# Low parts of the w_mlp_out weights: a negative from ScalarE and an adding transfer inside the SBUF, in place of VectorE's subtraction

## What is computed

```python
def _mlp(h, w_in, w_out):
    a = jnp.square(jax.nn.relu(h @ w_in))     # w_in 1024 x 4096
    return a @ w_out                          # w_out 4096 x 1024
```

## Time and profile before

| | |
|---|---|
| median of 3 runs | 1048.42 us |
| lowest, highest | 1047.06, 1050.18 us |
| the profiled execution | 1049.96 us |
| its span in the trace | 1048.0 us, 12487 instructions |
| mean granted TensorE clock | 0.977 |

### The profile page before, as it was taken

How to read it: one execution, slowest core, us unless ns; L and a number is a source line. 1 busy time by engine, 2 the same in 40 slices (tenths; PEclk the granted TensorE clock), 3 DMA queues, 4 the chain that set the end, 5 groups by cost and what they waited for, 6 DMA issues and landing times.

```text
span 1048.0 us, 12487 instructions
## 1 busy us (share of the span) xinstructions
PE 999.5 (95%) x4663; PEld 834.3 (80%) x4663; DVE 516.0 (49%) x815; ACT 407.4 (39%) x586; POOL 56.8 (5%) x40
## 2 busy tenths in 40 slices
PE   8916999999999999899999998999999999999998
PEld 7805888888888888688888887888888888888887
DVE  4804442313444151878888888574441314444221
ACT  7503432112334131656666666444441213433110
POOL 1100000000000000212222222000000000000000
PEclk9967999999999999999999999999999999999999
DMA  6652423232232323122222222142323233232231
GB/s 223 97 61 73 121 80 121 81 121 80 81 120 80 121 81 84 47 71 72 70 70 70 70 90 80 43 119 81 120 81 121 81 107 94 80 119 82 81 121 40
DMA packets 82667, 95.13 MB, mean 91 GB/s; under 512 B 3065, under 2 KB 61482, under 8 KB 82634
## 3 DMA queue, kind: packets, MB, share of 16 engines
q1 hardware_dynamic: 80954, 89.95, 27.4%
q0 software_dynamic: 1680, 4.72, 3.1%
HBM read 89.94 MB, written 4.72 MB: 90 GB/s over the span
## 4 chain that ended last, share of the span: by engine, by line
PE 89%; DVE 5%; another core or an unknown queue 3%; ACT 1%; issue 1%; DMA 1%; SPq 0%; DVEq 0%
PE bank L1081 28%; PE bank L1083 28%; PE bank L1082 28%; PE bank L1255 2%; PE bank L1285 1%; DVE w_low L717 1%; DMA work<-in_x_dram 1%; DVE h_low_buf L726 1%; DVE a_low_buf L726 1%; DVE work L738 1%; ACT w_high L457 1%; DVE work L908 0%; DVE neg_max L944 0%; DVE work L854 0%
## 5 line engine op out<-in xcount | busy, mean ns | idle before, releaser
L717 DVE TENSOR_TENSOR w_low<-raw,w_high 128x2048 fp32r<-128x2048 f32 (+1 forms) x75 | 163.3, 2177 | 268.0 <-ACT w_high L457 267.9
L1081 PE MATMUL bank<-h_high_buf,w_high 128*128 128x512 f32 x640 | 252.7, 395 | 0.0
L457 ACT ACTIVATE w_high<-raw 128x2048 fp32r<-128x2048 f32 (+1 forms) x77 | 140.1, 1819 | 288.8 <-PE bank L1083 254.7
L1083 PE MATMUL bank<-h_high_buf,w_low 128*128 128x512 f32 x640 | 250.5, 391 | 0.0
L1082 PE MATMUL bank<-h_low_buf,w_high 128*128 128x512 f32 x640 | 250.5, 391 | 0.0
L1081 PE MATMUL bank<-a_high_buf,w_high 128*128 128x512 f32 x528 | 207.6, 393 | 3.8 <-DVE a_low_buf L726 3.7
L1083 PE MATMUL bank<-a_high_buf,w_low 128*128 128x512 f32 x528 | 206.5, 391 | 0.0
L1082 PE MATMUL bank<-a_low_buf,w_high 128*128 128x512 f32 x528 | 206.3, 391 | 0.0
L1083 PEld LDWEIGHTS bank<-h_high_buf,w_low 128*128 128x128 f32 x640 | 120.8, 189 | 25.5
L1081 PEld LDWEIGHTS bank<-h_high_buf,w_high 128*128 128x128 f32 x640 | 121.1, 189 | 25.0 <-DVE h_low_buf L726 0.4
L1082 PEld LDWEIGHTS bank<-h_low_buf,w_high 128*128 128x128 f32 x640 | 121.1, 189 | 24.5
(11 more groups left out here) (130 smaller groups left out, 872.4 us busy)
## 6 DMA issues: line engine op xcount, KB each, us to landing
raw<-in_w_mlp_in_dram SPq DMA_DIRECT2D x32, 1024.0 KB, 5.5
raw<-in_w_mlp_out_dram SPq DMA_DIRECT2D x32, 1024.0 KB, 5.0
raw<-in_w_kv_dram SPq DMA_DIRECT2D x16, 512.0 KB, 4.0
raw<-in_w_q_dram SPq DMA_DIRECT2D x8, 512.0 KB, 5.3
raw<-in_w_o_dram SPq DMA_DIRECT2D x3, 1024.0 KB, 4.9
bias_by_distance<-work POOLq DMA_DIRECT2D x1, 2560.0 KB, 54.1
work<-in_x_dram SPq DMA_DIRECT2D x4, 512.0 KB, 5.3
work<-bias_by_distance POOLq DMA_DIRECT2D x8, 256.0 KB, 2.9
```

Source lines behind the costliest of these rows:

```text
L457: act.activation(w_high_buf[s][:, 0:cols], raw[s][:, 0:cols], ACT.Copy).then_inc(w_high, 1)
L717: dve.tensor_tensor(w_low_buf[s][:, 0:cols], raw[s][:, 0:cols], f32(w_high_buf[s][:, 0:cols]), ALU.subtract)\
L1081: pe.matmul(acc, w_hi, m_hi, start=start, stop=False)
L1083: return pe.matmul(acc, w_lo, m_hi, start=False, stop=stop)
```

## The change

For the 32 units of w_mlp_out (places 8 to 15 in each half), VectorE no longer subtracts. ScalarE, right behind its copy of the high part, writes the negative of the high part into the low buffer; it is the same copy with scale -1. GpSimd waits for that and issues one transfer inside the SBUF which adds the whole raw unit onto the low buffer: -high + raw. VectorE waits for the transfer and then writes one number into `low_cell`, only to count `w_low` in the old order. Two semaphores take turns, by the parity of the unit's index among the 32. The loops over these units are written out, since the index must be a number. GpSimd issues the 16 transfers of layer 0 after the bias rows' write and before its work for the heads, those of layer 1 at the end of its program.

```diff
+        low_cell = sb("low_cell", [1, 32])
...
+        neg_high = sem("neg_high")
+        low_added = [sem(f"low_added{i}") for i in range(2)]
...
+        def out_index(u):
+
+            for l in range(2):
+                d = u - U_MLP[l]
+                if 0 <= d < 32 and d % 16 >= 8:
+                    return 16 * l + 8 * (d // 16) + d % 16 - 8
+            return None
...
+            def add_lows(l):
+                for half in range(2):
+                    for q in range(8):
+                        u = U_MLP[l] + 16 * half + 8 + q
+                        n = out_index(u)
+                        pool.wait_ge(neg_high, n + 1)
+                        pool.dma_start(w_low_buf[u % 2][:, :], raw[u % 2][:, :], accum_op=ALU.add).then_inc(low_added[n % 2], 16)
+
+            add_lows(0)
             pool.wait_ge(w_used, U_HEAD)
...
             split_low(POOL_UNITS[1 + H])
+            add_lows(1)
...
+            def split_unit(u):
+
+                split_high(u, u % 2, landed(u))
+                if out_index(u) is not None:
+                    act.activation(w_low_buf[u % 2][:, :], raw[u % 2][:, :], ACT.Copy, scale=-1.0).then_inc(neg_high, 1)
...
-                    with act.Fori(first, 4) as i:
+                    with act.Fori(first, 3) as i:
                         for j in range(2):
                             split_high(u0 + 1 + j + 2 * i, (u0 + 1 + j) % 2, landed(u0 + 1 + j, i))
                             hidden(c0 + 2 * j + 4 * i, 2 * j + 4 * i)
+                    for j in range(2):
+                        split_unit(u0 + 7 + j)
+                        hidden(c0 + 2 * j + 12, 2 * j + 12)
...
+            def low_unit(u):
+
+                n = out_index(u)
+                if n is None:
+                    split_low(u, u % 2)
+                else:
+                    dve.wait_ge(low_added[n % 2], 16 * (n // 2 + 1))
+                    dve.memset(low_cell[:, n:n + 1], 0.0).then_inc(w_low, 1)
...
-                            with dve.Fori(0, 2) as r:
-                                for j in range(2):
-                                    u = u0 + 8 + 4 * f + 1 + j
-                                    split_low(u + 2 * r, u % 2)
+                            for q in range(4):
+                                low_unit(u0 + 9 + 4 * f + q)
```

More of the change, by code:

```diff
@@ L521, in mlp @@
                             for q in range(4):
-                                split_high(u + q, (u + q) % 2, landed(u + q))
+                                split_unit(u + q)
                                 if q in (1, 2):
@@ L534, in mlp @@
                         else:
-                            with act.Fori(0, 2) as r:
-                                for j in range(2):
-                                    split_high(u + j + 2 * r, (u + j) % 2, landed(u + j, r))
+                            for q in range(4):
+                                split_unit(u + q)
             act.wait_ge(consts_ready, 1)
@@ L784, in mlp @@
                         first = 1
-                    with dve.Fori(first, 4) as i:
+                    with dve.Fori(first, 3) as i:
                         for j in range(2):
@@ L788, in mlp @@
                             hidden(u0 + j + 2 * i, n0 + j + 2 * i, c0 + 2 * j + 4 * i, 2 * j + 4 * i, j)
+                    for j in range(2):
+                        low_unit(u0 + 7 + j)
+                        hidden(u0 + j + 6, n0 + j + 6, c0 + 2 * j + 12, 2 * j + 12, j)
                     for f in range(NF):
@@ L792, in mlp @@
                             for q in range(3):
-                                split_low(u0 + 13 + q, (u0 + 13 + q) % 2)
+                                low_unit(u0 + 13 + q)
                         elif l == 1 and half == 1:
                             for q in range(4):
-                                split_low(u0 + 9 + q, (u0 + 9 + q) % 2)
+                                low_unit(u0 + 9 + q)
                                 if q in (1, 2):
```

## The result

The changed kernel takes 1099.22 us (median of 4 runs, 1096.71 to 1100.43) against 1048.05 (4 runs): **1.048 times as long, interval 1.046 to 1.051**, some 51 us. The forecast was 1135 in a range of 1063 to 1205. The span grew from 1048.0 to 1098.6 us, by 50.6.

The account below looks back on a forecast made before the run. TensorE's own rate, 10.88 us a unit, was taken as the bound, with a new chain of 12.7 us exceeding it. Stalls 68.6, clock 8 and overlap 10 gave 87 us on 1048.4: 1135 us, range 1063 to 1205.

Parts of the forecast that it names:

- The bound and the slack: w_mlp_out stages: only TensorE's rate decides, 10.88 us a unit; VectorE's 73 us of subtractions lie in 6.6 us idle slack.
- T: Issue to landing of one 1 MB adding transfer in SBUF, taken as 8.7 us; the new chain decides from 6.8.
- The chain: From TensorE's release to the next unit's start: copy, negative, transfer, memset, 4.1 + T, 12.7 us in all against 10.88.
- Units 8 and 9: First two w_mlp_out units of each half: stalls of 3.9 and 6.8 us, the latter from hidden chunks queued behind VectorE's wait.
- Steady units: Units 11 to 15 of each half: stalls of 1.8, 0.7, 1.1, 0.7 and 1.1 us; unit 10 none.
- The second half of layer 0: Squares and norm sums between units 13 and 14 make unit 14 about 6 us late; this half loses 20.3 us, others 16.1.
- The clock: TensorE at 1.2 GHz after five longer stalls (four before units 9, one before unit 14): 1.6 us each, 8 us.
- Overlap: Transfers beside the load of unit u+2, by up to 2.9 us: 10 us taken, between 0 and 30.
- The sum: Whole kernel: stalls 68.6, clock 8 and overlap 10 make 87 us on the 1048.4 median, 1135 us.
- The third rival: Transfers hidden altogether, T at or below 4: 1048 us, only 2 us left at units 9; chance 0.03.
- The fourth rival: Faster: third rival plus a gain at the 34.71 us start-up load wait at 48.83; below 1045, at best 1019; chance 0.02.

Follow-up runs that it names:

- The copying transfers: The changed kernel with the addition (accum_op=ALU.add) left out, so the transfers copy raw over the low buffer: 1054.64 us, ratio 1.0055.
- the best of the changed kernels: The changed kernel with VectorE's subtraction kept for units 8 and 9 and the other 24 transfers cut in two column halves: 1057.03 us, ratio 1.0081.

## Why the prediction was right, and where it was off

- **The bound and the slack**: right. The removed 73 us of VectorE gave nothing back, ScalarE's pass costs nothing by itself, and the change is decided by one chain against 10.88 us.
- **T**: the mis-sized term. I took 2.1 + 2 x 3.3 = 8.7; the median is 6.9. The factor of two was right (5.2 against 2.7 us of the engines), but a pass inside the SBUF takes 2.7 us and not the 3.3 of a load, and the part that doesn't grow with size is 1.5 (4.2 - 2.7) and not 2.1: 1.5 and twice 2.7 are 6.9. Of the 32 transfers 7 took 8.4 to 10.4.
- **The chain** 4.1 + T: the parts are 0.05, then 1.83 for the copy and 1.90 for the negative (I had 1.92 for each), 0.29 for GpSimd to get going (I had 0.05), and 0.11 from the landing to TensorE's first product (0.15): 4.2. With 6.9 it is 11.1. The form was right, and the small errors nearly cancelled.
- **Units 8 and 9**: the places, their cause and their order were right. TensorE stood for 2.5 us before unit 8 (3.9 forecast, 2.2 by the formula at 6.9) and 2.8 before unit 9 (6.8; unit 9 started 15.6 behind unit 8 where the formula at 6.9 has 15.95, but 1.9 of that time went into unit 8 itself at its lower clock). Moving the wait shows the queue's part, 16.7 us.
- **Steady units**: forecast 1.8, 0.7, 1.1, 0.7 and 1.1, 5.4 a half; measured 2.0 in the first half. That is T again.
- **The second half of layer 0**: 4.2 us above an ordinary half forecast, 4.6 measured. Unit 14's copy came 14.9 us behind unit 13's; ScalarE's idle time before the fourth square is 6.66 in place of 1.60, and TensorE stood for 3.6 us before unit 14. But part of the 4.6 is another thing, which I had put at nothing: the heads' first loads and the last transfer lay beside each other (10.7 and 10.4 us to landing), and ScalarE waited 11.2 for them.
- **The clock**: 1.6 us for five stalls, 8 in all. Behind its stall unit 9 lost 1.8, 3.3, 1.9 and 1.8 us in the four halves, 8.8 together, while the fifth stall, 3.6 us before unit 14, was followed by a window at 1.00. So the total came out and its parts did not: it was partly luck. That unit 8's loss is covered by unit 9's longer chain held, also in layer 1, where unit 8 lost nothing: unit 9 started 15.6 us behind unit 8 in every half.
- **Overlap**: 10 us were set for transfers beside a load. Unit 10's transfer, issued within 1.2 us of a load, landed after 9.2, 8.7, 8.5 and 10.0 us in the four halves, but at unit 10 TensorE is late anyway. Two other places do cost time, and the sum had named neither: the heads' first loads and, in the last half, the four stores beside unit 14's transfer. The runs don't put a price on the overlap as a whole.
- **The sum** at the measured T: units 8 and 9 give 2.2 + 5.1 and the clock 1.8, which with the 2.0 measured at the others is 11.1 a half against 11.0. So the steps stand, and T is the error. By the prediction's own slope, 20 us for each 1 us, the 1.8 us of T are just the 36 between 1135 and 1099; but that close a fit is luck. Worked through unit by unit at 6.9, the same formulas leave about 8.2 us of stalls in an ordinary half and 12 in layer 0's second, since most of the steady terms vanish: 37, with the 8 for the clock 45, with the 10 for overlap 55, so 1093 to 1103 (an estimate). The measured time lies between.
- **The third rival** was added up wrongly. At T = 4 the formula for unit 9 leaves 2.2 us in each half, 8.7 in all, and not 2, so "hidden" would have needed a T under 2. The copying transfers, at 4.2, lost 5.7 us.
- **The fourth rival**'s place was real and had nothing to do with the change: the load of unit 2 is late because of the bias rows' write.

## What to carry to other kernels

Before work is moved off an engine that isn't the bound, set the whole new chain, from the release of the buffer to the next consumer, against the time of one unit: here 2.3 us a unit were saved on VectorE, which stood idle for 8.6, and the chain grew by 6.8 us where the slack was 6.6. Look for what stands in the same engine's queue behind the new wait, at the seam between two phases above all; moving one wait past three instructions gave back a third of the loss. And read the largest single wait of the page first, whatever the change is about: cutting up and postponing one write, issued at 28 us and first read at 424, was worth 35.7 us. Last, look for what else is under way where the new transfer runs: four output stores beside one transfer were more than half of what was left in the best of the changed kernels.

## What the runs showed that I had not expected

- An adding transfer in the SBUF on GpSimd's queue: 6.9 us for 1 MB from issue to landing against 4.2 for the copy; GpSimd is busy 0.85 us in issuing it against 0.53. Halves of 512 KB issued 1.9 us apart land in 5.4 each.
- A stall's length doesn't tell what it costs in clock. Unit 8's stalls of 2.2 and 2.5 us in layer 0 were followed by 48 products in 12.8 and 12.9 us (granted clock 0.87), those of 2.2 in layer 1 by a clock of 1.00. Unit 9's stalls of 2.8 us in layer 0 cost 1.8 and 3.3: in the second half TensorE resumed at 363.6 at the 1.2 GHz level, and products stayed 0.43 us apart until 369.7. One of 3.6 us before unit 14 cost nothing.
- A write of 2560 KB from 8 partitions took 54 us and held a 1 MB load for 53. In pieces of 320 KB one lands in 13.5, and no w_mlp_in load takes longer than 12.2. The pieces aren't cheaper: with them the packets of GpSimd's queue take 9.2% of 1010.4 us of the 16 engines, and 3.1% of 1048.0 before.
